# Two-layer attention block: the bias table between the index projections, x first, transposes copied ahead of exponentials

## What is computed

```python
def hybrid_layer(x, ...):
    proj = rms_norm(x, norm_g) @ w_in            # q, k, v of all branches, index q/k/w, gates
    y_a = stick_breaking_attention(sa_q, sa_k, sa_v)
    y_b = causal_softmax_attention(q_b, k_b, v_b, (MLA_NOPE + MLA_ROPE) ** -0.5)
    y_c = dsa_attention(...)
    ...
    return x + merged @ w_out

def dsa_attention(q, k, v, ix_q, ix_k, ix_w, positions, rel_bias):     # a block of 128 queries
    s_idx = relu(einsum('bqhd,bkd->bqhk', iq, ixk) * IDX_DIM ** -0.5)
    score = einsum('bqh,bqhk->bqk', iw * IDX_HEADS ** -0.5, s_idx)
    _, sel = lax.top_k(where(causal, score, -inf), topk)
    bias = rel_bias[t5_bucket(pq[:, :, None] - pk)]      # 32 buckets of distance, 8 heads
    logits = einsum('bqhd,bqkd->bqhk', qb, kg) * dh ** -0.5 + moveaxis(bias, -1, 2)
    p = softmax(where(valid, logits, -inf)); return einsum('bqhk,bqkd->bqhd', p, vg)
```

## Time and profile before

| | us |
|---|---|
| median of 3 runs | 1379.31 (1378.16 to 1379.43) |
| the profiled execution | 1379.81 |
| its span, first to last instruction | 1378.1 |
| around the span | 1.7 |
| PE busy | 1287.8 |
| start of the first projection | 76.75 |
| start of sa_v in layer 0 | 129.34 |

### The profile page before, as it was taken

The page is one execution under the profiler, slowest core; times in us unless marked ns, Lnnn a source line. Parts: engine busy times, 40 slices in busy tenths (PEclk is TensorE's granted clock), DMA queues, the critical chain, the costliest instruction groups (busy, mean ns, idle before and its releaser), DMA issues.

```text
span 1378.1 us, 17854 instructions
## 1 busy us (share of the span) xinstructions
PE 1287.8 (93%) x6530; PEld 971.6 (71%) x6538; DVE 775.8 (56%) x1582; ACT 608.3 (44%) x1130; POOL 181.3 (13%) x302
## 2 busy tenths in 40 slices
PE   3589999999889999999999999999988999999998
PEld 2277767656558888888888776665555888888887
DVE  7956577778653333354436667777855323435442
ACT  3335456666564223223324455666656322323330
POOL 3400111123330000000000021112333000000000
PEclk9899999999989999999999999999999999999999
DMA  6432221110241322222332311110024133232321
GB/s 167 115 115 84 70 62 32 46 31 1 81 135 31 122 92 92 92 92 92 101 83 92 93 62 62 33 54 22 17 74 126 50 104 92 92 95 90 121 93 61
DMA packets 118424, 109.15 MB, mean 79 GB/s; under 512 B 34496, under 2 KB 101056, under 8 KB 118336
## 3 DMA queue, kind: packets, MB, share of 16 engines
q1 hardware_dynamic: 110096, 107.96, 26.1%
q10 hardware_dynamic: 8240, 0.03, 0.3%
HBM read 100.64 MB, written 7.34 MB: 78 GB/s over the span
## 4 chain that ended last, share of the span: by engine, by line
PE 74%; DVE 10%; ACT 7%; issue 5%; POOL 2%; SPq 1%; DMA 0%; DVEq 0%; ACTq 0%
PE bank L736 19%; PE bank L738 19%; PE bank L737 19%; PE bank L844 2%; PE bank L1037 2%; PE bank L1010 2%; PE bank L1053 2%; DVE probs L1874 1%; POOL reach L466 1%; PE bank L868 1%; DVE w_lo L637 1%; ACT soft L1333 1%; PE bank L1066 1%; ACT soft L1335 1%; PE bank L885 1%
## 5 line engine op out<-in xcount | busy, mean ns | idle before, releaser
L736 PE MATMUL bank<-h_hi,w_hi 128*128 128x512 f32 (+1 forms) x928 | 360.1, 388 | 3.6 <-DVE h_lo L1567 2.2
L738 PE MATMUL bank<-h_hi,w_lo 128*128 128x512 f32 (+1 forms) x928 | 352.7, 380 | 0.0
L737 PE MATMUL bank<-h_lo,w_hi 128*128 128x512 f32 (+1 forms) x928 | 352.6, 380 | 0.0
L637 DVE TENSOR_TENSOR w_lo<-raw,w_hi 128x2048 fp32r<-128x2048 f32 (+2 forms) x98 | 187.7, 1916 | 129.0 <-ACT w_hi L631 128.9
L631 ACT CAST w_hi<-raw 128x2048 fp32r<-128x2048 f32 (+2 forms) x100 | 159.3, 1595 | 118.7 <-PE bank L738 118.7
L736 PEld LDWEIGHTS bank<-h_hi,w_hi 128*128 128x128 f32 x928 | 175.7, 189 | 46.9 <-issue 9.4
L738 PEld LDWEIGHTS bank<-h_hi,w_lo 128*128 128x128 f32 x928 | 175.7, 189 | 33.5
L737 PEld LDWEIGHTS bank<-h_lo,w_hi 128*128 128x128 f32 x928 | 175.7, 189 | 32.5 <-issue 1.9
L1508 ACT ACTIVATE gate<-bank,gains 128x512 f32<-128x512 f32 x48 | 33.0, 688 | 166.1 <-PE bank L738 166.1
L2019 POOL TENSOR_SCALAR probs<-probs,stat 128x128 f32<-128x128 f32 (+3 forms) x128 | 75.4, 590 | 167.7 <-DVE stat L1829 162.1
L1037 PE MATMUL bank<-mats,probs 128*128 128x128 f32 x320 | 57.7, 298 | 18.3 <-ACT probs_dsa L1481 18.3
(11 more groups left out here) (221 smaller groups left out, 2184.9 us busy)
## 6 DMA issues: line engine op xcount, KB each, us to landing
raw<-in_w_in SPq DMA_DIRECT2D x56, 1024.0 KB, 5.2
raw<-in_w_branch SPq DMA_DIRECT2D x12, 1024.0 KB, 5.1
raw<-in_w_out SPq DMA_DIRECT2D x8, 1024.0 KB, 5.1
bias<-bias_dram SPq DMA_DIRECT2D x16, 256.0 KB, 3.0
bias<-bias_dram SPq DMA_DIRECT2D x16, 192.0 KB, 2.6
x_sb<-in_x SPq DMA_DIRECT2D x4, 512.0 KB, 5.1
bias_dram<-bias_out SPq DMA_DIRECT2D x8, 256.0 KB, 2.9
raw<-in_w_in SPq DMA_DIRECT2D x4, 512.0 KB, 4.6
```

The costliest lines, as they stand in the source:

```text
L637: e.tensor_tensor(w_lo[:, s % RING, a:b], raw[:, s % RAW, a:b], w_hi[:, s % RING, a:b].bitcast(F32), ALU.subtract).then_inc(*lo_signal(nam ...
L736: pe.matmul(out_ap, lh, rh, start=start and i == 0, stop=False)
L737: pe.matmul(out_ap, lh, rl, start=False, stop=False)
L738: mm = pe.matmul(out_ap, ll, rh, start=False, stop=stop and i == n - 1)
```

## The change

Layer 0's start is reordered. x is loaded first, block by block with a signal each; `rel_bias` and one set of gains are loaded from ACT's queue, the other gains from SP's queue after the last bias store. Of the bias table only G 0-7 are made at the start, with `xn` and the transposes among them; the other 24 go into six slots of PE's index stage (`G_AT`), and of these POOL makes one reach in 4 instead of one in 8. The last slots use PSUM banks of the index scores, so all six groups of index scores come after the table. Layer 1's index stage is unchanged. In both layers, ACT copies the transposes of step j-2 ahead of the exponentials of j from j = 3 on, and the first logits of the DSA softmax no longer wait for the last exponentials of MLA.

```diff
+FIRST_G = 8
+G_AT = {"k_pe": (8, 11), "ix_q0": (11, 14), "ix_q1": (14, 17), "sa_q0a": (17, 22), "sa_q0b": (22, 27), "sa_q1a": (27, 32)}
...
         def on_pool(g):
-            return g % 8 == 7
+            return g % 8 == 7 or (g >= 4 * FIRST_G and g % 4 == 3)
+        def reach_tile(g):
+            if g < 4 * FIRST_G:
+                return reach_narrow[:, g % 8, :]
+            return (reach_v if g % 8 < 4 else reach_u)[:, g % 4, :]
...
             w = P * (g // 32 + 1)
-            if g >= 8:
-                e.wait_ge(*bias_mm.at(g - 8))
+            if 4 * FIRST_G <= g < 4 * FIRST_G + 8:
+                e.wait_ge(*bias_mm.of(0, 4 * FIRST_G - 1))
+            elif g >= 8:
+                e.wait_ge(*bias_mm.of(0, g - 8))
+            if g == 4 * FIRST_G + 7:
+                e.wait_ge(*x_turned.of(0, SEQ[-1], 1))
...
@@ SyncE
+            load_x(SEQ[0])
             e.dma_start(pos_i[:], ...)
             e.dma_start(mats[:], ...)
+            e.dma_start(gain_row[:], ...)
+            for s in SEQ[1:]:
+                load_x(s)
             load(SLABS[0])
             load(SLABS[1])
+            e.dma_start(take_f[:], ...)
...
+            store_bias(0, FIRST_G)
+            load(SLABS[2])
+            store_bias(8, 11)
+            load(SLABS[3])
+            store_bias(11, 17)
+            load(SLABS[4])
+            store_bias(17, GROUPS)
+            load(SLABS[5])
+            load_later_gains()
...
@@ TensorE
+            bias_groups(0, 4)
+            turn(SEQ[0])
+            bias_groups(4, 8)
+            turn(SEQ[1])
...
                 project("k_pe", "small", 0, P, SMALL, rows=second).then_inc(*dense.tick("k_pe"))
+                bias_slot("k_pe")
                 project("ix_q0", "ix_q", 0, P, rows=second).then_inc(*dense.tick("ix_q0"))
+                bias_slot("ix_q0")
                 project("ix_q1", "ix_q", P, P, rows=second).then_inc(*dense.tick("ix_q1"))
+                bias_slot("ix_q1")
...
+                if layer.l == 0:
+                    use("sa_q0")
+                    project("sa_q0", "sa_q0", 0, P, part=0)
+                    bias_slot("sa_q0a")
+                    project("sa_q0", "sa_q0", 0, P, part=1).then_inc(*dense.tick("sa_q0"))
+                    pe.wait_ge(*dve_evac.at("ix_q1"))
+                    take_heads((0, 1))
+                    bias_slot("sa_q0b")
+                    project("sa_q1", "sa_q0", P, P, part=0)
+                    take_heads((2, 3))
+                    bias_slot("sa_q1a")
+                    project("sa_q1", "sa_q0", P, P, part=1).then_inc(*dense.tick("sa_q1"))
+                    take_heads((4, 5))
...
+                    index_scores(0)
+                    use("sa_k0")
+                    project("sa_k0", "sa_k0", 0, P, part=0)
+                    take_heads((6, 7))
+                    index_scores(1)
+                    project("sa_k0", "sa_k0", 0, P, part=1).then_inc(*dense.tick("sa_k0"))
+                    index_scores(2)
+                    project("sa_k1", "sa_k0", P, P, part=0)
+                    index_scores(3)
+                    project("sa_k1", "sa_k0", P, P, part=1).then_inc(*dense.tick("sa_k1"))
+                    index_scores(4)
+                    index_scores(5)
...
                     elif u >= N_MLA:
-                        pe.wait_ge(*probs_exp.at(N_MLA - 1 if u % 2 else N_MLA - 2))
+                        pass
...
@@ ScalarE
                 e.activation(k_sq[64:96, :], dbank("k_pe")[64:96, :], ACT.Square)...
+                if layer.l == 0:
+                    bias_copies(8, 9)
                 hi(2)
...
+                    bias_copies(*G_AT["sa_q1a"])
+                    copy_sa("sa_q", 1)
+                    copy_parts(e, 4)
+                    index_relus(0)
+                    copy_parts(e, 6)
+                    hi(4)
+                    index_relus(1)
...
+                    if DSA_AV <= j < DSA_STEPS + DSA_T:
+                        turned_dsa()
                     if j < DSA_STEPS:
                         for u, o, h, t in dsa_units(j):
                             exp_of(u)
...
+                    if j == DSA_T:
+                        turned_dsa()
...
@@ VectorE
+            reaches(e, 0, 2)
+            xn_of(SEQ[0])
+            reaches(e, 2, 4)
+            xn_of(SEQ[1])
+            reaches(e, 4, 8)
+            h_lo_of(SEQ[0])
+            xn_of(SEQ[2])
+            h_lo_of(SEQ[1])
+            xn_of(SEQ[3])
+            angles(e)
             split_lo(e, SLABS[1])
...
+            reaches(e, 8, 10)
...
+                if layer.l == 0:
+                    reaches(e, 10, G_AT["ix_q0"][1])
+                    ix_q_parts(0)
+                    reaches(e, *G_AT["ix_q1"])
+                    ix_q_parts(1)
...
+                if layer.l == 0:
+                    reaches(e, *G_AT["sa_q0a"])
+                    copy_parts(e, 1)
+                    reaches(e, *G_AT["sa_q0b"])
+                    split_lo(e, SLABS[3])
+                    copy_parts(e, 3)
+                    reaches(e, *G_AT["sa_q1a"])
+                    copy_parts(e, 5)
...
+                    if layer.l == 0 and u == 4:
+                        copy_parts(e, 7)
+                    if layer.l and u == 4 or u == 14:
                         split_lo(e, SLABS[3 if u == 4 else 4])
...
@@ GpSimd
+            reaches(e, 0, 8, pool=True)
+            split_lo(e, SLABS[0])
+            reaches(e, 8, GROUPS, pool=True)
```

## The result

| | before | after |
|---|---|---|
| median of 14 runs each, us | 1378.63 | 1381.10 |
| lowest and highest | 1376.78, 1380.38 | 1378.89, 1385.26 |
| the profiled execution, its span | 1379.81, 1378.1 | 1382.60, 1380.9 |
| start of sa_v, layer 0 | 129.34 | 149.39 |
| first logits of the DSA softmax, layer 0 | 358.46 | 380.94 |

The ratio is 1.0023, with a 95% interval of 1.0014 to 1.0032: slower by 2 to 4 us, where 6.8 us less was forecast. The time lies in the range, the sign is wrong. The table says how. The index stage of layer 0 ends 20 us late (22.7 once sa_v's own first part, of which 5.4 us run at the low clock, is through), each DSA softmax gives some 10 us back, and the stages between pass the shift on. So both parts were far larger than forecast, +22.7 for +4 and -19.7 for -11, and nearly cancel.

A forecast was written before the change was run, and what follows sets the result against it. PE was taken as the bound, busy 1287.8 of 1378.1 us, with gains only at the start and in the DSA softmax. 1379.8 + 4 - 11 = 1372.8, given as 1372.5 us against the median; 8-in-10 range 1362 to 1385.

The forecast's parts named there:

- The sum: Layer 0's index stage: head start, PE work, stalls and tail added up to sa_v starting at 133.0 us, then 129.3.
- Part 1: Start and index stage of layer 0: moving 24 of 32 bias groups into the index stage costs 4 us.
- the tail: End of the index stage: the relu and score chain ends 22 us after take_heads 4 and 5, 5 us stall.
- The head start: Start of layer 0: with fewer bias groups there, k_pe ends at 46 us instead of 91.7, 45.7 us ahead.
- The work of 36.5 and 16 us: Index stage: PE's 36.5 us from k_pe to sa_v stay, and the moved bias groups add 16 us.
- rival 1: Index-stage slots: PE's clock falls in the slots of five, costing 12 us with slower POOL, 1384 us; chance 0.15.
- Stalls in the first slots: Slots behind k_pe: 7.0 us idle before group 10, 1.7 low clock, 1.2 and 1.6 at groups 13 and 16; 11.5 together.
- Stalls in the slots of five: Three index-stage slots of five bias groups: PE waits for POOL's successive reaches and DVE's held-back ones, 18 us.
- Rival 4: Slots of the index stage: POOL and DVE exclude each other, 9 us more, 1381.5 us; chance 0.03.
- Part 2: DSA softmax, both layers: copies ahead of exponentials remove PE's gaps and low clock, saving 5.5 us a layer, 11 us.
- rival 3: DSA softmax: PE becomes the bound, all six stretches fall to 10.5 us, some 22 us saved, 1361 us; chance 0.13.
- The sign: Whole kernel: faster, at 1372.5 us; chance 0.56 of faster by over 2.8 us, 0.27 slower, 0.17 the same.

The follow-up runs named there:

- bias_on_sp: Changed kernel with the eight `rel_bias` loads on SP's queue ahead of x instead of on ACT's queue; 1374.28 us, 0.9977 of before.
- dve_reaches: Changed kernel with DVE making all reaches of groups 8 to 31, between the projections, and POOL none; 1371.18 us, 0.9949 of before.
- g10_later: Changed kernel with bias group 10 moved from the slot after k_pe to the next one; 1377.51 us, 0.9992 of before.
- best2: Changed kernel with `rel_bias` on SP's queue, no POOL reaches between projections, group 10 a slot later, and three DVE reorderings; 1347.17 us.
- pool_extra: dve_reaches plus 24 reach-like POOL instructions in the same stretch, on a tile nobody reads; 1376.95 us, 0.9989 of before.
- one_in_eight: Changed kernel with POOL making one reach in eight between the projections instead of one in four; 1380.84 us, 1.0023 of before.

## Why the prediction was wrong, step by step

**The sum.** Part 1 was forecast at +4 us and cost 22.7. sa_v starts at 149.4 where the sum had 133.0, and the 16.4 us between are: k_pe's end 9.4 late, the three slots of five with the waits ahead of them 5.7 too short, the other work and stalls between k_pe and the tail 1.8, and the tail -0.5. Another 2.7 is the low clock at the start of sa_v, where the sum had none. The steps that failed are thus the landing of the `rel_bias` loads, which was put at nothing, POOL's reaches in the slots, which were taken to run beside DVE's, and the low clock, which was confined to two places.

**The head start: failed.** "The `rel_bias` loads leave from ACT's queue, of which I assume that they land as before" was the one assumption of that paragraph, and it cost 7.8 us of the 9.4 by which k_pe ended late (55.4 for 46). `bias_on_sp` shows it: with the loads on SP's queue k_pe ends at 46.8. The rest of DVE's line was sized well: ix_q's low part is ready at 42.9, 8.5 us later than forecast.

**The work of 36.5 and 16 us: right as a count, wrong in the clock and in the pace.** The same matmuls were busy for 14.4 us longer, by the estimate above 8.7 of them by the clock. The pace was the other part: a bias group was put at PE's own 0.43 to 0.87 us, and even in `dve_reaches`, where the slots of five are at full clock and free of POOL, the groups of 512 follow one another in 1.58 us, which is four of DVE's reaches. For the clock, I had put ix_q0's first half and 1.7 us behind group 10 at the low clock and everything else at the full one. In the trace the low clock also covers k_pe's first half and two stretches in the slots, 3.4 and 6.8 us long, each behind an idle time in which PE waits for POOL. That is rival 1's mechanism. It had 0.15, and speaking against it I had the table before, where PE was busy 16.7 of 25.9 us at full clock. That one stretch does not carry over. Nor does the length of a single idle time decide by itself: the 2.9 us ahead of a bias group before were not followed by the low clock, the 2.4 and 3.2 us after were. What the runs show is the price: for 7.6, 3.4 and 8.2 us less of idle time, `dve_reaches`, `g10_later` and `best2` have PE busy for 5.2, 3.7 and 5.0 us less, between 0.6 and 1.1 times as much again, most of it the clock's.

**Stalls in the first slots: right for group 10** (7.0 forecast, 6.35 measured), nothing for groups 13 and 16 (2.8 forecast, none over 0.8).

**Stalls in the slots of five: too small, and wrong in kind.** The slots last 7.4, 12.0 and 13.3 us, together 32.7, and with the 1.24 and 1.29 us in which PE waits for DVE ahead of the second and third, which the forecast counted in, 35.2, where 11.5 of work and 18 of stall make 29.5. POOL's reaches do not take 2.25 to 2.51 each: while the second slot runs they take 2.76, 2.38 and 3.62, in the third 5.37, 1.99 and 1.99. Two are held out by DVE, and the ones behind them start that much later. Rival 4 named that and had 0.03, because the earlier trace rows show both engines at work at once. But the trace of before had the other case too, behind a mean. The 2342 ns of the earlier trace rows for a width of 384 are the mean of four reaches of which one is this, in the timeline of POOL before:

```profile
46.37 4.17 POOL L466 TENSOR_SCALAR reach<-pos_f,edge 128x384 f32<-128x384 f32 x1 [16.41 <-PE bank L694]
```

It lies beside the last nine of the 21 reaches that DVE makes from 42.09 to 49.09, ends 1.45 us after them, and is what PE waits for in the 2.91 us at 50.59. I took the mean for a duration. The Trainium skill ("SBUF — State Buffer", "SBUF: two separate sides") has the port pair that VectorE and GpSimd share as an exclusive lock: of a GpSimd instruction and a VectorE one of the kinds that take the pair, whichever starts first holds it for the whole instruction. The traces agree in that POOL, where shut out, finished 1.86 us after DVE's run ended and no sooner, and in that POOL's presence lengthened DVE's reaches by 7.7 us in `pool_extra`. They don't agree on the whole instruction: there POOL's of 2.22 us at 111.20 lies beside five of DVE's reaches, none longer than 0.93 us.

**The tail: right.** From the end of take_heads 4 and 5 at 127.9 to sa_v it took 21.5 us, where 22 were forecast, 4.1 of it idle where 5 were. These two rows are the end of take_heads and the start of sa_v:

```profile
127.49 0.41 PE L892 MATMUL bank<-ix_q_lo,take 32*128 32x512 f32 x2
149.39 0.80 PE L839 MATMUL bank<-w_hi,h_hi 128*128 128x512 f32 x1 [1.86 <-ACT ix_relu L1387]
```

Stores, slabs and later gains held nobody up, as forecast.

**Part 2: the mechanism right, one term mis-sized.** The gaps in front of the transposes went and the step without a split came down to 9.7 (10.3 forecast). The stretches with the weight split were the error: 12.1 and 12.2 for 14.1. I had put both splits of four steps into the chain, 3.8 us; measured is 2.4 or 2.5 more than without a split. In the first of the two PE is busy 11.6 of 12.1 us, at a clock of 0.86, so there PE is the bound, as in rival 3, which had 0.13; the second has PE busy for 10.05 of 12.2 and is still the chain's. With those terms corrected, 2.0, 1.9 and 0.6 us more saved a layer, 5.5 becomes 10.0; measured 9.5 and 10.2.

**The sign.** Two errors of 19 and 9 us in opposite directions hid one another in the time, and the range held for that reason. The price in it for what was assumed about the loads was nil; it should have been bounded by the landing of x, which shares the DMA engines.

What stays open: whether the low clock alone, at unchanged gaps, has the price that I read from the busy times (no run held PE busy through a gap); what brings it down; and why POOL gets its turn among DVE's reaches in most slots of `pool_extra` and is shut out in `one_in_eight`.

## What to carry to other kernels

Where two engines share, read the single durations and not their mean, and look at what the other did beside the longest one; then ask whether the change makes that case common. Cost an idle time of PE at its length and at what the matmuls behind it lose by the clock, here 0.6 to 1.1 times as much again in PE's busy time. And a small load that many wait for did better here ahead of the large ones on the same queue than on another queue beside them, by 6 us.

## What the runs showed of the hardware

- The last of eight 1 KB loads on ACT's queue was in use 10.8 us after its issue, beside 512 KB loads on SP's queue; on SP's queue ahead of them the last was in use at 5.29 us.
- A reach of 512 on POOL takes 1.99 us alone, 2.2 to 2.8 where it got its turn among DVE's reaches, and 3.4 to 7.4 where it was shut out; then it ends 1.85 to 1.87 us after DVE's run. Beside DVE's copies out of PSUM it was not slowed: one of 384 took 1.56 us there and 1.56 alone.

```profile
76.28 1.56 POOL L513 TENSOR_SCALAR reach_u<-pos_f,edge 128x384 f32<-128x384 f32 x1
...
87.32 1.56 POOL L513 TENSOR_SCALAR reach_v<-pos_f,edge 128x384 f32<-128x384 f32 x1
```

- In return DVE's reaches of 512 went from 480 to 627 ns in the mean. Single ones show how: beside one instruction of POOL that got its turn, two or three of DVE's took 0.82 to 0.93 us and the others 0.47 to 0.48.
